# Moving the loads of kept weight halves from the sync queue to ScalarE's queue in a hybrid encoder step

## The reference, cut to what matters

```python
h = rmsnorm(x, norm_mix_g[l])
u = jnp.einsum('btd,dc->btc', h, w_in[l]).astype(f32)
a_gate, a_x, b_z, b_xbc, b_dt, c_qkv, c_z, c_beta, c_a, d_u = _split_cols(u)
...
mix = jnp.concatenate([y_a, y_b, y_c, y_d], axis=-1).astype(x.dtype)
x = x + jnp.einsum('btc,cd->btd', mix, w_out[l])
x = x + cross_attend(rmsnorm(x, norm_cross_g[l]), mem_k, mem_v, w_cq[l], w_co[l])
x = x + swiglu(rmsnorm(x, norm_ffn_g[l]), w_ffn_gate[l], w_ffn_up[l], w_ffn_down[l])
```

## Time and profile before

| | |
|---|---|
| median of 3 runs | 4240.63 us (4239.75 to 4242.36) |
| the profiled execution's own time | 4238.34 us |
| its span (first to last instruction) | 4236.5 us |
| PE busy | 3748.2 us, 88% of the span |
| PEld busy | 3627.6 us, 86% |
| DVE, ACT, POOL busy | 2228.1, 1255.2, 320.8 us |
| mean granted TensorE clock | 0.927 of full speed |
| DMA | 942 MB, 222 GB/s on average |

### The profile page before, as it was taken

How to read it: one execution, slowest core, us unless ns; L and a number is a source line. 1 busy time by engine, 2 the same in 40 slices (tenths; PEclk the granted TensorE clock), 3 DMA queues, 4 the chain that set the end, 5 groups by cost and what they waited for, 6 DMA issues and landing times.

```text
span 4236.5 us, 63633 instructions
## 1 busy us (share of the span) xinstructions
PE 3748.2 (88%) x24250; PEld 3627.6 (86%) x24250; DVE 2228.1 (53%) x4752; ACT 1255.2 (30%) x2291; POOL 320.8 (8%) x340
## 2 busy tenths in 40 slices
PE   5587868898788899997899997899998899998998
PEld 5586867798788899997899997899998799998998
DVE  7576644167773545563555554554455455543323
ACT  4344332145432322222323232323232322322101
POOL 0010000001100001100101100001010001100000
PEclk8798977689999999998999998999999999999999
DMA  7755585479968456567555666556666655566776
GB/s 246 239 170 175 175 299 209 130 266 364 350 247 275 163 195 220 206 219 251 191 195 210 220 221 220 208 197 210 212 223 221 216 177 206 199 212 246 244 251 216
DMA packets 372574, 942.08 MB, mean 222 GB/s; under 512 B 35120, under 2 KB 168752, under 8 KB 371760
## 3 DMA queue, kind: packets, MB, share of 16 engines
q1 hardware_dynamic: 372272, 938.03, 63.6%
HBM read 763.32 MB, written 174.57 MB: 221 GB/s over the span
## 4 chain that ended last, share of the span: by engine, by line
PE 54%; DVE 16%; DMA 11%; PEld 6%; DVEq 4%; ACT 3%; issue 3%; SPq 2%; ACTq 0%; PEldq 0%
PE banks L441 15%; PE banks L442 14%; PE banks L443 14%; DMA uc_dram<-uc_sb 3%; DVE m_p_sb L2073 2%; DMA kept_dram<-wlo_sb 2%; DMA wlo_sb<-kept_dram 2%; PEld banks L443 2%; DVE uc_sb L1131 2%; PEld banks L441 2%; PEld banks L442 2%; PE banks L1512 1%; PE banks L1518 1%; DVE wlo_sb L1040 1%; PE banks L1521 1%
## 5 line engine op out<-in xcount | busy, mean ns | idle before, releaser
L441 PE MATMUL banks<-hh_sb,whi_sb 128*128 128x384 f32 (+2 forms) x3552 | 1216.0, 342 | 162.2 <-DVE wlo_sb L1040 58.1
L442 PE MATMUL banks<-hh_sb,wlo_sb 128*128 128x384 f32 (+2 forms) x3552 | 1181.8, 333 | 0.0
L443 PE MATMUL banks<-hl_sb,whi_sb 128*128 128x384 f32 (+2 forms) x3552 | 1180.2, 332 | 0.0
L441 PEld LDWEIGHTS banks<-hh_sb,whi_sb 128*128 128x128 f32 x3552 | 696.6, 196 | 193.1 <-issue 69.1
L442 PEld LDWEIGHTS banks<-hh_sb,wlo_sb 128*128 128x128 f32 x3552 | 697.1, 196 | 2.1 <-issue 1.2
L443 PEld LDWEIGHTS banks<-hl_sb,whi_sb 128*128 128x128 f32 x3552 | 696.0, 196 | 0.0
L441 PE MATMUL banks<-g_hi_sb,whi_sb 128*128 128x384 f32 (+2 forms) x1568 | 541.9, 346 | 77.6 <-DVE g_lo_sb L1151 30.1
L442 PE MATMUL banks<-g_hi_sb,wlo_sb 128*128 128x384 f32 (+2 forms) x1568 | 528.4, 337 | 0.0
L443 PE MATMUL banks<-g_lo_sb,whi_sb 128*128 128x384 f32 (+2 forms) x1568 | 528.3, 337 | 0.0
L441 PEld LDWEIGHTS banks<-g_hi_sb,whi_sb 128*128 128x128 f32 x1568 | 316.5, 202 | 91.2 <-DVE g_lo_sb L1151 33.3
L1232 DVE TENSOR_TENSOR x_sb<-x_sb,banks 128x384 f32<-128x384 f32 (+2 forms) x400 | 202.4, 514 | 330.9 <-PE banks L443 327.4
(11 more groups left out here) (411 smaller groups left out, 5143.7 us busy)
## 6 DMA issues: line engine op xcount, KB each, us to landing
whi_sb<-kept_dram SPq DMA_DIRECT2D x560, 512.0 KB, 3.7
wlo_sb<-kept_dram SPq DMA_DIRECT2D x560, 512.0 KB, 4.8
raw_sb<-w SPq DMA_DIRECT2D x144, 512.0 KB, 5.0
kept_dram<-whi_sb SPq DMA_DIRECT2D x112, 512.0 KB, 6.5
kept_dram<-wlo_sb SPq DMA_DIRECT2D x112, 512.0 KB, 7.3
uc_dram<-uc_sb SPq DMA_DIRECT2D x90, 192.0 KB, 3.4
ldb_sb<-x_t SPq DMA_DIRECT2D x72, 192.0 KB, 4.6
x_sb<-x_t SPq DMA_DIRECT2D x5, 1536.0 KB, 9.2
```

What stands on the lines that cost most here:

```text
L441: eng.matmul(out, xh, yh, start=first, stop=False)
L442: eng.matmul(out, xl, yh, start=False, stop=False)
L443: return eng.matmul(out, xh, yl, start=False, stop=last)
```

## The change

`sp_kept` becomes `act_kept`, with the same wait and the same two DMAs. ACT calls it in `act_section`, behind the splits of first-use halves and in front of all other work of the section, for the same uses as SP did. SP's section no longer has it. Nothing else changes: KEPT_AHEAD, the slots and the waits of PE are as before.

```diff
+        def act_kept(eng, n):
+            slot_free(eng, n)
+            first = W_KEPT_USE[W_LOAD[n]]
+            eng.wait_ge(w_kept[first % SPLITS], 32 * in_slot(W_KEPT, first))
+            for part, w in enumerate((whi, wlo)):
+                eng.dma_start(w[n % SPLITS][:, 0:W_WIDTH[n]].bitcast(F32),
+                              kept_dram[W_LOAD[n], part, :, 0:W_WIDTH[n]]).then_inc(w_loaded[n % SPLITS], 16)
+
         def act_section(eng, i):
...
             act_splits(eng, min(N_W, before + SPLIT_AHEAD) if i else 0, min(N_W, s.after + SPLIT_AHEAD))
+            for n in range(min(N_W, before + KEPT_AHEAD) if i else 0, min(N_W, s.after + KEPT_AHEAD)):
+                if W_LOAD[n] >= 0:
+                    act_kept(eng, n)
             act_second(eng, i - 1)
...
             sp_weights(eng, min(N_W, before + LOAD_AHEAD) if i else RAWS, min(N_W, s.after + LOAD_AHEAD))
-            for n in range(min(N_W, before + KEPT_AHEAD) if i else 0, min(N_W, s.after + KEPT_AHEAD)):
-                if W_LOAD[n] >= 0:
-                    sp_kept(eng, n)
```

More of the change, by code:

```diff
@@ L1270, in pool_section @@
                 eng.tensor_tensor(g, g, rstd[:, unit.ni % 2, 0:cols(unit.p)], ALU.mult).then_inc(gs_done, 1)
[L1274 to L1281, removed]
         def sp_keep(eng, n):
```

## The result

The changed kernel takes 4265.42 us (median of 7 runs, 4261.08 to 4286.37) where the kernel before takes 4242.0 us beside it. The ratio is 1.0061, with a 95% interval of 1.0044 to 1.0079: slower by 0.6%, or 26 us. The prediction said 4227 us, 14 us faster. The profiled execution took 4268.28 us, its span is 4266.4 us, 29.9 us more than before.

A forecast was written before the change was run, and what follows sets the result against it. PE bounds the kernel, save for a DMA-bound stretch of some 60 us at each change from stage A to B. The terms -44 - 21 + 36 + 15 + 0 gave -14 us: about 4227 us, range 4212 to 4234.

The forecast's parts named there:

- Part 1: Mainly around stage A: kept loads no longer behind SP's other work, shortening PE's 52.1 us of waits; -44 us.
- Part 2: End of stage A: `z_dram` stores no longer stand behind kept loads, 4.2 us in each of 5 rounds; -21 us.
- (b): Rival: the store doesn't get past the loads on the shared DMAs, Part 2 gives 0, Part 1 half; 4270 us, chance 0.10.
- Part 3: FFN, `s` and other sections: kept loads now wait for ACT, held by mixer steps or x, and come late; +36 us.
- Part 4: `w` sections at the start of stage B: SP issues the mixer's 1408 KB sooner, taking DMA time from kept loads; +15 us.
- Part 5: Issuing 570 loads moves 430 us of queue time to ACT, where it falls into idle time; 0 us.
- (a): Rival: ACT comes too late with the loads, Part 3 at its upper bound of 75 us; 4266 us, chance 0.22.

The follow-up runs named there:

- e5: Kernel before, but ACT begins the kept loads of `u` and `z` sections, at earlier places in its list; SP begins all others; 4216.58 us, ratio 0.9932.
- e6: Kernel before, SP still beginning all kept loads, but those of `u` and `z` sections at earlier places in its list; 4219.27 us, ratio 0.9942.
- e9: Changed kernel, but ACT begins the kept loads of the FFN (`g`, `up`, `d`) one section earlier; 4251.36 us, ratio 1.0014 to the kernel before.
- e3: Changed kernel, but SP keeps its old slot waits at `w` sections, so the mixer's loads go out late; 4256.78 us, ratio 1.0036 to the kernel before.
- e1: Kernel before, but ACT begins the kept loads in front of `u` and `z` sections (108 of 570), SP the others; 4225.13 us, ratio 0.9962.
- e8: Kernel before, with the kept loads of 16 `g` sections begun late on purpose; 4305.84 us, ratio 1.0142.
- e10: e5 with one load per pass, that of the second `w` section, moved behind the `z_dram` stores; 4224.2 us, ratio 0.9945 to the kernel before.
- e11: e6 with one load per pass, that of the second `w` section, moved behind the `z_dram` stores; 4229.87 us, ratio 0.9964 to the kernel before.

## Why the prediction was wrong

**Part 1, the failed step: -44, measured about -15.** The `u` and `z` sections gained 15.5 us. Of the 52.1 us of waits for kept loads 43.7 lay in them, and 25.5 were left. The prediction took nearly all of the 52.1 us of waits for kept loads, though its own reading at 1961 us had found ACT only half a microsecond ahead of SP. It set its hope on DVE's wait for `uc_dram` stores, to shrink by 1.5 to 3 us for each store of a row. It shrank by 1.7 us in all there (6.12 to 4.45), and 11 us over the kernel (88.5 to 77.5). The load then took 2 us longer to land, and PE's 4.76 us became 3.86. The queue that was to be free, ACT's, waits at that spot for the same thing, and the store that DVE waits for landed only 0.6 us sooner without a kept pair of SP's in front of it. e5 and e6 show what those waits depended on: the place of the load in the list. The prediction had no such case among its four rivals.

**Part 2: -21, measured -8.3.** The place was right and the size too large. The store took 7.40 us for 9.12 and not 2 to 4, since it still landed behind the 2 MB begun ahead of it, by 0.2 us, as it had by 0.4 us with all of them in one queue. The sum also counted five rounds; of ACT's five waits for `z_dram` four were 6.4 to 7.5 us and the first 1.1 us. ACT's wait fell to 25.3 us, not under 10, and PE's 7.19 us to 4.46, not 3. Rival (b) had this half right.

**Part 3: +36, measured 36.0** (27.1 in the FFN, 4.0 in `s`, 4.9 in the last pass). The sum is right for the wrong reasons. Of the 36, 11 were for the step of line 1819 in three rounds; there the waits came to 12.4 us, near enough. But it held loads at two more sections, in a fourth round, and 8 of the 27.1 us are slow clock behind the waits, which no term priced. The 18 us for some 20 other loads mostly didn't come. The place in the last pass, where ACT stands at the square of x, wasn't seen at all. e9 confirms the FFN term at 20 us.

**Part 4: +15, measured 13.2** in the traces and 11 us by e3. Right in place, cause and size.

**Part 5: 0.** The 110 `g` sections of passes 1 to 5 got 0.7 us longer in all, but for the one counted in the FFN row, and an issue costs 0.33 and 0.46 us on ACT. PE's wait for ACT's exponentials (line 956) rose from 13.8 to 19.7 us, and is 15.6 us in e1; a few us of the `s` row may be this part.

**The rivals.** The time, 4265, is the one that (a) gave, 4266, but not by its mechanism: landing times stayed, waits for kept loads stayed under 100 us, and late loads cost what part 3 had for them. It was the gain that failed, as in (b), whose 4270 us is as near and whose reason, that the store doesn't get past the loads, explains part 2 and a piece of part 1. That the time fell on (a)'s figure is luck. With parts 1 and 2 at what they measured, the prediction's own sum is -15 - 8 + 36 + 15 = +28 us, and the trace shows +29.7.

## What to carry to other kernels

Before moving a transfer to another engine's queue, look at what that engine's own list waits for at the same spot; if both wait for the same event, it is the place in the list that counts, and here moving the transfer ahead in the old queue gave as much. Split such a change by stage: here one half alone was worth 16 us and the other alone cost 61, though together they cost 26. And a freed queue begins other transfers sooner, which can be priced from the order of the two kernels.

## What the runs showed of the hardware

A wait of PE cost more than its length where it stood: 48.8 us of waits made their sections 71.7 us longer (e8), since the granted clock fell to half behind 14 of the 16, and in the changed kernel for 5.9 us behind a wait of 4.40; the two sections without such a stretch got no such tail. Over the whole kernel the cost was 52 us in the profiled execution and 60 us (50 to 70) by the ratio, and the mean granted clock didn't change. The fall isn't decided by the wait's length alone: in the changed kernel 3.56 us were followed by a clock of 0.55, and 3.55 us at the same step of the next round by 1.00. What decides stays open.

A 128 KB store took 9.1, 7.4 and 5.6 us in three arrangements of the loads around it, and in each it landed 0.2 to 0.4 us behind the last load begun ahead of it, whether SP or ACT had begun that load. The kept load of the third `w` section took 7.9 or 4.8 us depending on 1408 KB begun just ahead of it. In time the choice of queue made no difference that these runs can tell (e5 and e6, e10 and e11).
